# Experts with one extra block come last and their extra blocks run from the weights already in place: a hybrid decoder step on one core

## The reference, cut to what matters

```python
g_star = jnp.argmax(lg, axis=-1)                     # 1 of 4 groups
top_v, top_i = lax.top_k(le_g, TOP_K_IN_GROUP)       # 2 of its 8 experts
eid = g_star[:, None] * EXP_PER_GROUP + top_i
...
hid = silu(einsum('nd,edf->nef', xf, w_gate)) * einsum('nd,edf->nef', xf, w_up)
y = einsum('nef,efd->nd', hid * comb[..., None], w_down)
```

## Time and profile before

| | |
|---|---|
| median of 3 runs | 822.17 us (819.4 to 822.24) |
| profiled execution, its own time | 821.36 us |
| its span in the trace | 819.5 us |
| PE, DVE, ACT, POOL busy | 94%, 45%, 24%, 21% of the span |
| mean granted clock of PE | 0.983 |
| bytes moved | 140.05 MB, a mean of 171 GB/s |

### The profile page before, as it was taken

One profiled execution on the slowest core, in us unless ns is written; L12 is line 12 of the kernel. 1 busy time (PEld: TensorE's weight loads), 2 busy tenths in 40 slices (PEclk: granted clock), 3 DMA queues, 4 the chain that ended last, 5 costly groups with the idle time before them and its releaser, 6 DMA issues.

```text
span 819.5 us, 11726 instructions
## 1 busy us (share of the span) xinstructions
PE 772.4 (94%) x4589; PEld 540.2 (66%) x4589; DVE 371.3 (45%) x790; ACT 199.9 (24%) x435; POOL 170.7 (21%) x270
## 2 busy tenths in 40 slices
PE   5999999999999989999999999999999999998674
PEld 3657778878666667777767777774457855655431
DVE  2201999895488869103026632232137522232106
ACT  3000112131456651215226530000010112222114
POOL 2338548030000015000025220001000212232100
PEclk9999999999999999999999999999998999999878
DMA  9785545178000016521135359508007789999746
GB/s 310 173 30 189 157 104 149 45 218 281 2 1 2 1 32 177 180 77 52 51 85 162 117 148 319 215 1 290 31 26 286 283 325 412 408 403 386 310 158 242
DMA packets 91922, 140.05 MB, mean 171 GB/s; under 512 B 29909, under 2 KB 64881, under 8 KB 90703
## 3 DMA queue, kind: packets, MB, share of 16 engines
q1 hardware_dynamic: 75855, 102.46, 36.8%
q0 software_dynamic: 11392, 32.71, 13.8%
q10 hardware_dynamic: 4616, 4.08, 1.6%
HBM read 133.04 MB, written 21.14 MB: 188 GB/s over the span
## 4 chain that ended last, share of the span: by engine, by line
PE 85%; DVE 6%; DMA 5%; SPq 1%; issue 1%; ACT 1%; ACTq 0%; DVEq 0%; POOL 0%; POOLq 0%
PE ps L1925 18%; PE ps L2117 15%; PE ps L2457 7%; PE ps L2379 7%; PE ps L1949 5%; PE ps L2025 4%; PE ps L2473 3%; DMA arena<-w_up 2%; PE ps L2160 2%; PE ps L2135 2%; PE ps L2148 2%; PE ps L2447 2%; PE ps L2407 2%; DMA arena<-yscratch 2%; PE ps L2221 1%; PE ps L2003 1%
## 5 line engine op out<-in xcount | busy, mean ns | idle before, releaser
L2117 PE MATMUL ps<-xT,keep 128*128 128x288 f32 x512 | 126.9, 407 | 0.8 <-ACT h L1226 0.5
L2117 PEld LDWEIGHTS ps<-xT,keep 128*128 128x128 f32 x512 | 96.5, 190 | 27.4 <-ACT h L1226 0.9
L1925 PE MATMUL ps<-xT,arena 128*128 128x288 f32 x384 | 95.6, 408 | 1.1 <-DVE keep L1508 1.1
L1925 PEld LDWEIGHTS ps<-xT,arena 128*128 128x128 f32 x384 | 72.1, 190 | 20.7 <-issue 1.4
L1415 DVE SCALAR_TENSOR_TENSOR cv<-keep,cv 128x512 f32<-128x512 f32 x120 | 83.6, 746 | 1.4
L2379 PE MATMUL ps<-arena,xT 128*128 128x512 f32 x128 | 55.4, 592 | 0.0
L1000 POOL TENSOR_SCALAR keep<-keep,pmod 128x64 f32<-128x64 f32 x16 | 7.8, 508 | 176.2 <-PE ps L2160 120.0
L2379 PEld LDWEIGHTS ps<-arena,xT 128*128 128x128 f32 x128 | 24.2, 190 | 29.3 <-issue 29.2
L2457 PE MATMUL ps<-keep,mgT 128*64 128x256 f32 x224 | 41.7, 389 | 1.7 <-DMA mgT<-w_up 1.5
L1949 PE MATMUL ps<-mgT,xT 128*128 128x512 f32 (+1 forms) x128 | 43.3, 497 | 0.0
L1045 POOL DMA_INDIRECT yscratch<-cv,slots_of x19 | 19.0, 1001 | 100.2 <-PE ps L2447 67.2
(11 more groups left out here) (411 smaller groups left out, 1331.9 us busy)
## 6 DMA issues: line engine op xcount, KB each, us to landing
arena<-w_down SPq DMA_DIRECT2D x19, 512.0 KB, 16.2
keep<-w_in SPq DMA_DIRECT2D x16, 512.0 KB, 3.9
arena<-w_gate SPq DMA_DIRECT2D x15, 512.0 KB, 7.8
arena<-w_up SPq DMA_DIRECT2D x15, 512.0 KB, 10.8
keep<-w_gate SPq DMA_DIRECT2D x14, 512.0 KB, 10.1
keep<-w_up SPq DMA_DIRECT2D x14, 512.0 KB, 17.5
h<-x_prompt SPq DMA_DIRECT2D x8, 512.0 KB, 5.7
arena<-w_in SPq DMA_DIRECT2D x8, 512.0 KB, 8.7
```

The costliest lines, as they stand in the source:

```text
L1925: last = mm(tokens(j)[:, b, :], weights(k), halves(x[:, k, :])[:, b, :], start=k == 0, stop=k == n_k - 1)
L2117: last = mm(out[:, 0:half], wmg[n // 2 % 3][:, k, :], xT[:, k, (n % 2) * half:(n % 2 + 1) * half], start=k == 0, stop=k == KD - 1, skip_gr ...
```

## The change

1. Experts with exactly one extra block and a number from 11 on (those whose weights aren't loaded before the routing is known) get the last places among the 32; the other experts keep their order and close the gaps. The first of them gets place 31, the second place 30, and so on. DVE computes the place of each expert (`place64`, 64 times the place) and the inverse table, place to expert, which goes into `eid`.
2. SP reads the expert of each slot from 11 on out of that table (`placed`).
3. The order of the steps is pairs 0 to 15, then 18, 17, 16. The extra block of the expert at place 31 is block 32, that of place 30 is block 33, and so on; extra blocks of other experts come after these. A slot with extra block 32 + n uses the home of place 31 - n (`home_w`), and where its expert lies there, nothing is loaded (`resident`).
4. The owners of the extra blocks are computed inside the loop, after DVE's part of step 2 (`owners_of_blocks`).

```diff
-MID = 8
-STEPS = list(range(MID)) + list(range(NE // 2, NUSUAL)) + list(range(MID, NE // 2))
+STEPS = list(range(NE // 2)) + list(range(NUSUAL - 1, NE // 2 - 1, -1))
...
+        def home_w(x):
+
+            over = block_of(x) - NE
+            return (NE - 1 - over if 0 <= over < KEPT and x < 2 * NUSUAL else x) % HOMES_W
+
+        def in_home(x):
+            return [y for y in range(x) if home_w(y) == home_w(x)]
...
+            def placed(x):
+                at = sp.value_load(eid[0:1, 2 * N_OVER + x:2 * N_OVER + x + 1], min_val=0, max_val=NE - 1)
+                return None, bass.ds(at, 1)
+
             def freed(x, what):
-                take(sp, J_MOE + 4 * ((x - HOMES_W) // 2) + what)
-
-            more_of = {}
+                take(sp, J_MOE + 4 * (in_home(x)[-1] // 2) + what)
+
+            asked = {}
 
             def next_gate_up(x):
-                if blocks_of(x // 2) < NE // 2:
-                    freed(x, 1)
-                    gate_up(x)
+                asked[x] = used, e = placed(x) if x < NE else over(x)
+                freed(x, 1)
+                if x < NE:
+                    gate_up(x, e)
                     return
-                more_of[x] = used, e = over(x)
-                freed(x, 1)
                 sp.nop(nofuse=True)
                 with sp.If(used < NE):
                     gate_up(x, e)
                 with sp.Else():
-                    sp.sem_inc(s_we[x % HOMES_W], 32)
+                    sp.sem_inc(s_we[home_w(x)], 32)
...
+            sp.wait_ge(s_eid, 1)
             for x in range(HOMES_W, 2 * NUSUAL):
-                if x == 2 * MID:
-                    sp.wait_ge(s_eid, 2)
+                if x == NE:
+                    sp.wait_ge(s_eid, 3)
                 next_gate_up(x)
...
-            st.do(V.tensor_tensor_scan(run[:, 1:], one_e, n_over, 0.0, ALU.mult, ALU.add))
-            st.do(V.scalar_tensor_tensor(shift, run[:, 0:NE], float(BR), over_at, ALU.mult, ALU.add))
-            st.do(V.scalar_tensor_tensor(by_tile(jump), by_tile(at), float(BR), shift.unsqueeze(1).to_broadcast([P, NT, NE]), ALU.is_ge, ALU.mult))
-            give(V.tensor_tensor(at_place, jump, at, ALU.add), J_POS)
+            st.mark(V.tensor_tensor_scan(run[:, 1:], one_e, n_over, 0.0, ALU.mult, ALU.add))
+            st.do(V.scalar_tensor_tensor(kept, n_over, 1.0, may_keep, ALU.is_equal, ALU.mult))
+            st.mark(V.tensor_tensor_scan(kept_run[:, 1:], one_e, kept, 0.0, ALU.mult, ALU.add))
+            st.mark(V.scalar_tensor_tensor(other_shift, run[:, 0:NE], float(BR), over_at, ALU.mult, ALU.add))
+            st.do(V.tensor_tensor(moved, kept, from_end, ALU.mult))
+            st.mark(V.tensor_scalar(other_shift, other_shift, kept_run[:, NE:NE + 1], None, ALU.add))
+            st.do(V.tensor_tensor(moved, moved, kept_run[:, 0:NE], ALU.subtract))
...
+            st.do(V.tensor_tensor(place64, moved, e_row, ALU.add))
...
+            def owners_of_blocks():
...
+                for half in range(2):
...
+                    st.mark(V.tensor_tensor(owner, by_block(shift), number, ALU.is_le))
+                    st.do(V.tensor_tensor(ended, by_block(place64), number, ALU.is_le))
+                    st.do(V.tensor_tensor(owner, owner, ended, ALU.subtract))
+                    st.do(V.tensor_tensor(owner, owner, by_block(e_no), ALU.mult))
+                    st.do(V.tensor_reduce(owners[:, n], owner, AX.X, ALU.add))
...
                     gate_up(p)
                     if p + 2 < p1:
                         put_rows(p + 2)
+                    if p == 2:
+                        owners_of_blocks()
```

More of the change, by code:

```diff
@@ L359, in build, with room @@
         xeT = [cut(ROUTING + 1024 * s, KD, P, base=mg_flat) for s in range(2)]
-        given = [ROUTING]
-        def room(*shape):
+        cv_flat = cv[:, :, :].rearrange("p a b -> p (a b)")
+        AHEAD = 11
+        EARLY, KEPT_ROOM, BESIDE = [ROUTING, ROUTING + 2 * D, mg_flat], [ROUTING + 2 * D, 2 * KD * T, mg_flat], [NT * (BR + 3 * NBLK), CC * T, cv_flat]
+        def room(*shape, where=EARLY):
             n = 1
@@ L379, in build @@
         group_share, pair_share = room(NT), room(NT)
-        run, owners = room(NE + 1), room(N_OVER)
-        cv_flat = cv[:, :, :].rearrange("p a b -> p (a b)")
+        run, kept_run = room(NE + 1, where=KEPT_ROOM), room(NE + 1, where=KEPT_ROOM)
+        owners, missing, resident = (room(N_OVER, where=KEPT_ROOM) for n in range(3))
+        owner, ended = (room(N_OVER // 2, NE, where=KEPT_ROOM) for n in range(2))
         ye = [cut(1024 * s, D, base=cv_flat) for s in range(2)]
@@ L401, in build, with blocks_of @@
         so_far = room((NT + 1) * NE // 2).bitcast(BF16)
-        e_no, g_no, one_e, over_at = (room(NE) for n in range(4))
-        n_over = room(NE).bitcast(I32)
-        row_at, shift = room(2 * NT), room(NE)
+        e_no, n_over_words, shift, place64 = (room(NE, where=KEPT_ROOM) for n in range(4))
+        n_over = n_over_words.bitcast(I32)
+        g_no, one_e, over_at, kept, may_keep, from_end, other_shift, moved, shift_less = (room(NE) for n in range(9))
+        def blocks_of(p):
+            return STEPS[p] if p < NUSUAL else p
         WU = D
@@ L782, in next_gate_up @@
                 with sp.Else():
-                    sp.sem_inc(s_we[x % HOMES_W], 32)
+                    sp.sem_inc(s_we[home_w(x)], 32)
             def next_down(x):
+                used, e = asked[x]
                 freed(x, 3)
-                if x not in more_of:
-                    down(x)
+                if x < NE:
+                    down(x, e)
                     return
-                used, e = more_of[x]
                 sp.nop(nofuse=True)
@@ L1836, in _ @@
             V.tensor_tensor(pair_exp, best[:, :, 1], best[:, :, 0], ALU.subtract).then_inc(s_sub, 1)
-            owner = grid.rearrange("p (n w) -> p n w", w=NE)
-            st.do(V.tensor_tensor(owner, run[:, 1:].unsqueeze(1).to_broadcast([P, N_OVER, NE]), blocks.unsqueeze(2).to_broadcast([P, N_OVER, NE]), ALU.is_le))
-            st.do(V.tensor_reduce(owners, owner, AX.X, ALU.add))
-            V.tensor_copy(eid[:, 0:N_OVER], owners).then_inc(s_eid, 1)
-            V.tensor_scalar(eid[:, N_OVER:], owners, float(NE - 1), None, ALU.min).then_inc(s_eid, 1)
+            late = NE - HOMES_W
@@ new lines, in _ @@
+            st.do(V.tensor_tensor(expert_at, place64.unsqueeze(1).to_broadcast([P, late, NE]), e_row[:, HOMES_W:].unsqueeze(2).to_broadcast([P, late, NE]), ALU.is_equal))
+            st.do(V.tensor_tensor(expert_at, expert_at, e_no.unsqueeze(1).to_broadcast([P, late, NE]), ALU.mult))
+            st.do(V.tensor_reduce(moved[:, 0:late], expert_at, AX.X, ALU.add))
+            V.tensor_copy(eid[:, 2 * N_OVER + HOMES_W:], moved[:, 0:late]).then_inc(s_eid, 1)
+            def owners_of_blocks():
+                by_block = lambda x: x.unsqueeze(1).to_broadcast([P, N_OVER // 2, NE])
+                st.do(V.tensor_tensor(shift, shift, place64, ALU.add))
+                st.mark(V.tensor_scalar(missing, blocks, run[:, NE:NE + 1], float(NE), ALU.is_ge, ALU.mult))
+                st.mark(V.tensor_scalar(resident[:, 0:KEPT], blocks[:, 0:KEPT], float(BR), kept_run[:, NE:NE + 1], ALU.mult, ALU.is_lt))
+                st.do(V.tensor_scalar(shift, shift, 1.0 / BR, -float(NE - 1), ALU.mult, ALU.add))
+                st.do(V.tensor_tensor(place64, shift, n_over, ALU.add))
+                for half in range(2):
+                    n = slice(half * N_OVER // 2, (half + 1) * N_OVER // 2)
+                    number = blocks[:, n].unsqueeze(2).to_broadcast([P, N_OVER // 2, NE])
+                    st.mark(V.tensor_tensor(owner, by_block(shift), number, ALU.is_le))
[3 more added lines that the diff above has]
+                    st.do(V.tensor_reduce(owners[:, n], owner, AX.X, ALU.add))
+                st.do(V.scalar_tensor_tensor(missing[:, 0:KEPT], resident[:, 0:KEPT], float(NE), missing[:, 0:KEPT], ALU.mult, ALU.add))
+                V.tensor_copy(eid[:, 0:N_OVER], missing).then_inc(s_eid, 1)
+                V.tensor_copy(eid[:, N_OVER:2 * N_OVER], owners).then_inc(s_eid, 1)
@@ L2453, in gates_ups @@
                 for x in (2 * p, 2 * p + 1):
[L2454 removed]
+                    pe.wait_ge(s_we[home_w(x)], 32 * (len(in_home(x)) + 1))
                 for k in range(KD):
                     for u in range(2):
[L2457 removed]
+                        last = mm(slot(j + 1)[u * BR:(u + 1) * BR, 0:2 * F], xeT[p % 2][:, k, u * BR:(u + 1) * BR], wgu[home_w(2 * p + u)][:, :, k, :],
                                   start=k == 0, stop=k == KD - 1)
@@ L2493, in _ @@
             experts(0, NUSUAL)
-            pe.wait_ge(s_eid, 2)
+            pe.wait_ge(s_eid, 3)
             more = more_blocks(pe)
```

65 lines of the change are left out of this document (35 added, 30 removed).

## The result

| | before | after |
|---|---|---|
| median of 11 runs each | 822.17 us (819.4 to 823.67) | 826.64 us (825.03 to 829.92) |
| ratio, 95% interval | | 1.0061 [1.0048, 1.0075] |
| profiled execution, its span | 821.36, 819.5 us | 826.64, 824.9 us |
| bytes moved | 140.05 MB | 135.34 MB |
| mean granted clock | 0.983 | 0.986 |

What follows compares the result with a forecast made beforehand. TensorE was taken as the bound till 746 us, then weight loads. Loop end +2.0 and clock 0.75 sum to +2.75 on the profiled 821.4 us, 824.1; 0.8 more for the median gives 824.9 us, range 817 to 829.

Steps and rivals of the forecast that it cites:

- the line of 0.5%: Whole kernel: 4.1 us either way (818.1 and 826.3) taken as no change; slower 0.31, same 0.54, faster 0.15.
- B: Rival, chance 0.16: fewer bytes win, step 15's load lands with TensorE ready, loop end -7.7, 814.5 us.
- points 5 and 6: End of loop: step 15 waits for the 21st load until 762.0, three whole steps follow, end 789.9, +2.0.
- point 3: Owners of blocks on DVE inside the loop: 5.8 us, TensorE waits 2.0 us once, vanishing in load waits.
- Points 2, 4 and 8: Table of experts by place (1.1 us, covered), SP's register loads per slot, 76 rows in the last scatter: nothing each.
- D: Rival, chance 0.13: the 21st load lands 1.0 to 2.3 us sooner, little queued behind it: 822.5 to 824.
- C: Rival, chance 0.18: expert 1's extra load, issued at 758, lands 775 to 776.5; if later, TensorE waits: 829.
- point 1: Routing chain on DVE: new instructions +1.5, tiles' choices -0.4, so the loop starts 1.1 us later; bounds 0.7 and 1.6.
- point 7: Clock after step 15's wait of 2.2 to 3.7 us: price 0 or 1.5, half taken, 0.75.
- point 6: Behind step 15's load: three whole steps, 19.4 us, then 8.5 undisturbed from step 18's start; end 789.9, +2.0.
- Steps 13 and 14: Late loop, waits for w_up: 17th load lands 741.1 with TensorE due 739.3; 19th lands 751.8 with step 14 ready 747.6.

Runs made afterwards that it cites:

- nores: Changed kernel with no extra block taken as resident, so 36 expert loads instead of 33: 828.1 us, 1.0070 of the kernel before.
- best_nores: Changed kernel with empty pair 18 behind pair 11, 56 filler transposes and owners in four pieces, but nothing resident, 36 loads: 824.32 us, 1.0022 of the kernel before.
- order_only: Kernel before with only the step order changed (pairs 0 to 15, then 18, 17, 16), no residence, 36 loads: 824.21 us, 1.0020.
- split: Changed kernel with the owners computed in four pieces, after steps 2, 3, 4 and 5: 828.22 us, 1.0075 of the kernel before.
- fill56: Changed kernel with 56 instead of 42 filler transposes ahead of TensorE's wait for the routing chain: 825.95 us, 1.0039 of the kernel before.
- plain_empty_mid: Kernel before with only its step order changed: empty pair 18 behind pair 11, pairs 17 and 16 last, 36 loads: 822.99 us, 1.0017.
- middle_all: Changed kernel with the three pairs of extra blocks behind pair 11 and nothing resident, 36 loads: 824.94 us, 1.0034 of the kernel before.
- best: Changed kernel with empty pair 18 behind pair 11, 56 instead of 42 filler transposes and owners in four pieces: 819.87 us, 0.9959 of the kernel before.

## Why the prediction was right, and what it missed

It said 824.9 us, the median is 826.64; the range 817.0 to 829.0 holds it. A small loss was forecast and came, 4.5 us instead of 2.75; but at +0.61% it lies past the line of 0.5% that I had given 0.31, and under it I had put 0.54.

**Right, and shown.** *Which bytes count.* 33 loads, and the last expert's binds: no step behind it waits for a load, and `nores` shows that making three more loads changes nothing that can be told. That is why B (814.5) fell. The Trainium skill (Perfetto Trace Analysis, Identifying the Most-Contended Engine) says to work first on the engine with the highest occupancy, and to judge DMAs by their bandwidth instead. From 740 to 760 us the DMAs are busy all the time, at 386 GB/s, and TensorE for 15.7 of 20 us; yet the three loads saved are worth nothing that can be told in `nores` and some 5 us in `best_nores`, so that alone didn't tell. *The cover gone (points 5 and 6).* Without the 1.1 of the loop start, my working gives 760.95 + 19.4 + 8.5 = 788.85, +0.9, and +1.65 with the 0.75 for the clock. `order_only` ends its loop at 789.48, +1.5, and its median is +2.0. *The owners (point 3).* 5.8 forecast, 681.88 - 675.84 = 6.0 measured, and TensorE waited 2.2 against 2.0, hidden, as `split` shows. *Points 2, 4 and 8.* The chain of the kernel after does pass through SP's reads, some 0.57 us a slot ahead of the last loads, but little of it reaches the end: from the inversion to step 15 `fill56` needs 119.5 us and `order_only`, which has no reads, no table and no owners in the loop, 119.2. The tail's 0.5 us is not explained and within what executions differ by. *D* came in small: in `order_only` the 21st load releases its step at 760.22, 0.7 us before 760.95.

**C was right in its first half.** The extra load of expert 1 was issued at 761.43 and 761.86, 3 to 4 us later than the 758 that I gave; but it landed in 9.3 us, not in 17 to 18.3, at 771.2, for a step that starts at 778.2. The queue ahead of it was nearly empty; the issue itself took 0.38 us. I had used landing times of a full queue (DMA share 1.00) for a stretch with 0.43.

**Mis-sized: point 1, the routing chain.** "The indices, the row gathers and, through TensorE's filler of 66 transposes, the loop start 1.1 us later" measured 653.49 - 650.33 = 3.16. The new instructions were nearly right: 2.90 us from scan to product instead of 1.20, +1.7 for +1.5 forecast. The 0.4 us that I took off for the tiles' shorter choices didn't come: from the product to the inversion it is 3.60 us in both kernels, and the inversion starts 1.5 us later. What I left out is what TensorE does while it waits for it: the wait grew from 0.7 to 2.42 us, the granted clock fell, and the 66 transposes behind it took 9.02 instead of 7.36. The first row is the kernel before, the other two after:

```profile
644.00:646.00 2.00, 2.00 (x21) 2.00 (x20) 1.81 (x9) 1.18 (x1) 1.37 (x2) 1.00 0.26 96
```
```profile
644.00:646.00 2.00, 2.00 (x12) 2.00 (x11) 1.83 (x9) 0.91 (x3) 0.16 (x1) 0.50 0.24 90
646.00:648.00 2.00, 2.00 (x14) 2.00 (x13) 1.90 (x5) 0.69 (x1) 1.69 (x2) 0.66 0.15 16
```

From 644 to 646 the clock is 1.00 with 21 matmuls before, 0.50 with 12 after. `fill56` takes the wait away, and the transposes take 7.36 again. Of the 3.16 us, 2.74 reach step 15, since every home is released that much later and the loads with it.

**The clock (point 7).** I took half of 1.5. Step 15's wait of 2.86 us cost the whole: 5.20 for 3.60, +1.6. But the step released late in the kernel before, step 18, had paid the same, so the two nearly cancel in the division above; that cancellation was in my 8.5 of point 6 as well. For this execution the Trainium skill's page (TensorE: Matmul & The Clock Gate, HAM oscillation), by which I had +3.5 for the sum, was nearer than my half. But the other runs don't bear out its "every". In one and the same execution of `plain_empty_mid` a wait of 3.54 us left the clock at 1.00 (first product 0.40 us) and one of 2.25 us didn't (0.66):

```profile
761.97 0.40 PE L2457 MATMUL ps<-mgT 128*64 128x256 f32 x1 [3.54 <-DMA keep<-w_up]
...
770.77 0.66 PE L2457 MATMUL ps<-keep,mgT 128*64 128x256 f32 x1 [2.25 <-DMA arena<-w_up]
```

Waits of 3.17 (`middle_all`) and 3.43 us (`split`) cost nothing either. So the length of the wait alone doesn't say what it costs, no run here shows what does, and that step 15 paid may be chance. My reading of the earlier trace rows, as if 1.5 and 3.1 us enclosed a border, was too simple.

**Steps 13 and 14.** Forecast waits 1.8 and 4.2, measured 4.3 and none. TensorE was ready for step 13 at 741.7 instead of 739.3, the 17th load landed at 745.9 instead of 741.1, and the products of step 13 ran slow behind the wait, 5.36 us; step 14's weights were there by then.

**The end of the loop, in the prediction's terms.** It gave 790.65 (789.9 and 0.75 for the clock), measured 792.86. Step 15 starts 1.7 us later than its 762.0, the clock takes 0.85 more, the last of the three steps is 0.5 shorter (6.01, where I had 6.48 for each), and the last stretch is 0.1 longer, 8.62 for 8.5.

The sum by measured terms: the order +2.0, everything else +2.8, 4.8 against 4.5 by the medians. Mine was 1.65 for the order and 1.1 for everything else, 2.75. With the reservation on `middle_all` above, most of what was missing is the loop start.

**Open.** How the 2.8 us of `middle_all` divide between the slow clock at the loop start (1.66) and the longer way to it (1.5, the rest of 3.16) was read from the traces alone; the time of `fill56` is too near that of after to settle it. What decides whether a wait costs the clock stays open too. Why `split` alone read higher than after, not lower, while `best` with the same split is among the fastest, isn't known; its interval overlaps that of after. And an order with two steps behind the last expert and expert 1's block in the middle wasn't tried.

## What to carry to other kernels

When a change saves transfers, ask which of them stand ahead of the load that releases a step: as long as that load binds, only those count, and the full steps behind that load are added whole, so light or empty steps belong ahead of it and not behind it. Saving the last loads pays once those bind, with few steps behind the last expert: the order, the residence and the shorter wait gave 0.9959 together, while the order alone gave 1.0017 and the residence without the order nothing that could be told. When a chain that a filled engine waits for gets longer, lengthen the filler by as much.

## What the runs showed of the hardware

- Five kernels have TensorE wait 2.4 us ahead of the 66 transposes; these then took 8.89 to 9.02 us, in the kernel after with a granted clock of 0.50 (1.2 GHz) from 644 to 646 us. In six kernels with a wait of 0.7 to 0.9 us they took 7.35 or 7.36. So the wait cost some 1.6 us on top of itself.
- Behind waits for weights the gate products came out both ways. After 2.25 (`plain_empty_mid`), 2.30 (`order_only`), 2.86 (after) and 3.40 us (`best_nores`) they started slow, 0.66 us for the first; after 1.50, 2.73 (`fill56`), 3.17 (`middle_all`), 3.43 (`split`) and 3.54 us (`plain_empty_mid`) they ran at full clock.
- The landing of one and the same kind of 512 KB load was 16.98 to 21.1 us with the queue full (slot 27 of the kernel after: issued 724.78, landed 745.9), 9.3 us in the emptied queue of the same kernel, and 7.51 us in `best_nores`. Taking a landing time from one stretch into another gave the miss in C.
